# A two-layer hybrid trunk on one core: the MLP loop's two products interleaved matmul by matmul

## The reference

```python
    h = rms_norm(x, g_pre_mlp)
    y = jnp.square(jax.nn.relu(h @ w_mlp_in)) @ w_mlp_out
    return x + rms_norm(y, g_post_mlp)
```

## Time and profile before

| | before |
|---|---|
| median of 3 runs | 802.89 us (802.56 to 804.55) |
| the profiled execution's own time | 802.94 us |
| its span in the profile | 801.2 us |
| TensorE (PE) busy | 788.9 us, 98% |
| VectorE (DVE) busy | 505.4 us, 63% |
| ScalarE (ACT) busy | 403.0 us, 50% |
| DMA read from HBM | 144.31 MB, 181 GB/s over the span |
| TensorE's granted clock, mean | 0.996 |

### The profile page before, as it was taken

One profiled execution on the slowest core, in us unless ns is written; L12 is line 12 of the kernel. 1 busy time (PEld: TensorE's weight loads), 2 busy tenths in 40 slices (PEclk: granted clock), 3 DMA queues, 4 the chain that ended last, 5 costly groups with the idle time before them and its releaser, 6 DMA issues.

```text
span 801.2 us, 11130 instructions
## 1 busy us (share of the span) xinstructions
PE 788.9 (98%) x4126; PEld 664.5 (83%) x4126; DVE 505.4 (63%) x698; ACT 403.0 (50%) x619; POOL 56.7 (7%) x88
## 2 busy tenths in 40 slices
PE   8999999999999999999999999999999999999997
PEld 6898787887888888888879887878878888888885
DVE  4588555459777656556575776545687765655663
ACT  5565555444455454444555655655436654444441
POOL 2010000006110000000020100000242000000000
PEclk9999999999999999999999999999999999999999
DMA  7796455654467565666556864555644676666631
GB/s 243 208 295 212 125 158 158 197 181 147 132 203 226 179 187 190 193 201 204 173 150 192 277 198 122 154 180 179 205 138 131 198 219 186 184 205 190 180 128 53
DMA packets 85404, 145.87 MB, mean 182 GB/s; under 512 B 4950, under 2 KB 50406, under 8 KB 85367
## 3 DMA queue, kind: packets, MB, share of 16 engines
q1 hardware_dynamic: 85334, 145.33, 59.0%
q0 software_dynamic: 32, 0.05, 0.0%
HBM read 144.31 MB, written 1.05 MB: 181 GB/s over the span
## 4 chain that ended last, share of the span: by engine, by line
PE 90%; DVE 4%; POOL 2%; ACT 2%; DMA 1%; issue 1%; POOLq 0%; DVEq 0%; ACTq 0%
PE banks L1180 21%; PE banks L1182 21%; PE banks L1181 21%; PE banks L1228 11%; PE banks L1229 6%; DVE w_lo L730 2%; PE banks L1232 2%; DMA raw<-in_w_in_dram 1%; PE banks L1192 1%; PE banks L1231 1%; PE banks L1276 1%; PE banks L1294 1%; PE banks L1238 1%; PE banks L1268 1%; ACT w_hi L447 1%
## 5 line engine op out<-in xcount | busy, mean ns | idle before, releaser
L730 DVE TENSOR_TENSOR w_lo<-raw,w_hi 128x1024 fp32r<-128x1024 f32 (+1 forms) x272 | 317.3, 1196 | 126.1 <-ACT w_hi L447 125.5
L447 ACT CAST w_hi<-raw 128x1024 fp32r<-128x1024 f32 (+1 forms) x272 | 266.2, 1015 | 121.8 <-PE banks L1182 49.8
L1180 PE MATMUL banks<-w_hi,xT_both 128*128 128x512 f32 (+2 forms) x480 | 182.3, 380 | 0.8 <-DVE xT_both L753 0.8
L1182 PE MATMUL banks<-w_hi,xT_both 128*128 128x512 f32 (+2 forms) x480 | 178.1, 371 | 0.0
L1181 PE MATMUL banks<-w_lo,xT_both 128*128 128x512 f32 (+2 forms) x480 | 178.1, 371 | 0.0
L1228 PE MATMUL banks<-xT_both,w_hi 128*128 128x512 f32 x392 | 140.6, 398 | 0.0
L1180 PE MATMUL banks<-w_hi,brT_hi 128*128 128x512 f32 x320 | 125.0, 390 | 0.0
L1181 PE MATMUL banks<-w_lo,brT_hi 128*128 128x512 f32 x320 | 124.5, 389 | 0.0
L1182 PE MATMUL banks<-w_hi,brT_lo 128*128 128x512 f32 x320 | 124.5, 389 | 0.0
L1229 PE MATMUL banks<-xT_both,w_lo 128*128 128x256 f32 x392 | 110.0, 281 | 0.0
L1180 PEld LDWEIGHTS banks<-w_hi,xT_both 128*128 128x128 f32 x480 | 90.5, 189 | 17.9 <-issue 2.9
(11 more groups left out here) (176 smaller groups left out, 698.5 us busy)
## 6 DMA issues: line engine op xcount, KB each, us to landing
raw<-in_w_in_dram SPq DMA_DIRECT2D x96, 512.0 KB, 4.5
raw<-in_w_mlp_in_dram SPq DMA_DIRECT2D x64, 512.0 KB, 4.8
raw<-in_w_mlp_out_dram SPq DMA_DIRECT2D x64, 512.0 KB, 4.3
raw<-in_w_branch_dram SPq DMA_DIRECT2D x16, 512.0 KB, 4.0
raw<-in_w_out_dram SPq DMA_DIRECT2D x16, 512.0 KB, 3.8
raw<-in_w_in_dram SPq DMA_DIRECT2D x16, 176.0 KB, 3.2
x<-in_x_dram SPq DMA_DIRECT2D x4, 256.0 KB, 4.5
gain_pre<-in_g_pre_mlp_dram SPq DMA_DIRECT2D x2, 512.0 KB, 6.0
```

The costliest lines, as they stand in the source:

```text
L447: nc.scalar.copy(w_hi[:, c % RING, h * n:(h + 1) * n], raw[:, q % RAW, 0:n]).then_inc(hi_ready, 1)
L730: v.tensor_tensor(w_lo[:, c % RING, cut], raw[:, q % RAW, 0:n], w_hi[:, c % RING, cut].bitcast(F32), ALU.subtract).then_inc(lo_ready, 1)
L1180: nc.tensor.matmul(dst, l_hi, r_hi, start=first, stop=False)
L1182: return nc.tensor.matmul(dst, l_lo, r_hi, start=False, stop=last)
```

## The change

The loop calls a new function, `mlp_in_and_out`, in place of `mlp_in` and `mlp_out`. It waits for both chunks of the block and for the hidden part of step k at its beginning, and then issues the same 32 input matmuls and 24 output matmuls in turns: one output matmul between the wide and the narrow one of each kt, and another one behind every second kt. `chunk_used` is counted at the last input matmul, which is the last but one of the block, and at the last output matmul, the last of the block; before, the first count came at the end of the input product, in the middle of the block.

```diff
@@ -1524,6 +1524,46 @@
                             elif last:
                                 mm.then_inc(y_psum, 1)
 
+                def mlp_in_and_out(k_in, k_out, c, i):
+
+                    wait_chunk(l, c, i)
+                    wait_chunk(l, c + 1, i)
+                    pe.wait_ge(hidden_lo_ready, nth(l, STEPS, k_out + 2 * i))
+                    hi, lo = both(c)
+                    out_hi, out_lo = both(c + 1)
+
+                    def output_matmul(q):
+
+                        t, h, j, term = q // 12, q // 6 % 2, q // 3 % 2, q % 3
+                        n = hidden_slot(k_out) + j
+                        a = (brT_lo if term == 1 else brT_hi)[:, n, tokens(t)]
+                        w = (out_lo if term == 2 else out_hi)[:, j, columns(h)]
+                        return nc.tensor.matmul(psum[:, 2 * t + h, :], a, w, start=False, stop=False)
+
+                    q = 0
+                    for f in range(2):
+                        bank = 4 + 2 * (k_in % 2) + f
+                        cut = slice(f * P, (f + 1) * P)
+                        for kt in range(KT):
+                            wide = (psum[:, bank, :], hi[:, kt, cut], xT_both[:, kt, :, :].rearrange("p b n -> p (b n)"))
+                            narrow = (psum[:, bank, 0:S], lo[:, kt, cut], xT_hi[:, kt, :])
+                            if kt < KT - 1:
+                                nc.tensor.matmul(*wide, start=kt == 0, stop=False)
+                                output_matmul(q)
+                                nc.tensor.matmul(*narrow, start=False, stop=False)
+                            else:
+                                nc.tensor.matmul(*narrow, start=False, stop=False)
+                                output_matmul(q)
+                                last = nc.tensor.matmul(*wide, start=False, stop=True)
+                                if f == 1:
+                                    last.then_inc(chunk_used, 1)
+                            q += 1
+                            if kt % 2 == 1:
+                                mm = output_matmul(q)
+                                q += 1
+                    assert q == 24
+                    mm.then_inc(chunk_used, 1)
+
                 mlp_in(2, C_IN2, f=0)
                 hidden_transposes(l, 1)
                 mlp_in(2, C_IN2, f=1).then_inc(chunk_used, 1)
@@ -1532,8 +1572,7 @@
                     for b in range(2):
 
                         pe.wait_ge(relu_ready, nth(l, STEPS, 1 + b + 2 * i))
-                        mlp_in(3 + b, C_LOOP + 2 * b, i).then_inc(chunk_used, 1)
-                        mlp_out(1 + b, C_LOOP + 2 * b + 1, i)
+                        mlp_in_and_out(3 + b, 1 + b, C_LOOP + 2 * b, i)
                 pe.wait_ge(relu_ready, nth(l, STEPS, STEPS - 3))
                 mlp_in(STEPS - 1, CHUNKS - 4).then_inc(chunk_used, 1)
                 for t in range(T):
```

## The result

Twelve runs on one chip, six of each kernel: the changed kernel 806.74 us (806.23 to 809.09), before 803.55 us (802.56 to 804.55). The ratio is 1.0048, with a 95% interval of 1.0033 to 1.0062: about 3.9 us, between 2.7 and 5.0. Executions of either kernel fall into two groups some 2 us apart, three and three of before's, four and two of the changed kernel's, which is why the medians differ by only 3.2 us. The forecast was 804.7 us and "no change that can be told" (0.55); it came out on the slow side (0.33), inside the range of 801.0 to 809.0.

A forecast was written before the change was run, and what follows sets the result against it. TensorE was taken to bound the kernel, busy 788.9 of 801.2 us. To 802.94 us the forecast added 0 for matmul intervals, 0 for waits inside the loop and 1.8 for its end: 804.7 us, range 801.0 to 809.0.

The forecast's parts named there:

- no change that can be told: Whole kernel: time within about 0.3%, 2.4 us, of before, called "the same"; chance 0.55.
- Part 1: MLP loop: the number of wide, narrow and output matmuls per block stays as before; cost 0.
- Part 2: MLP loop: 14 steps from narrow to wide per block before and after, so the interval between matmuls stays; 0 us.
- The rule from the Trainium skill: MLP loop: loads and matmuls together set the spacing; output matmuls around narrow ones would remove the mixing price, 2.2 us less.
- Part 3: Inside the loop: earlier waits and later releases leave VectorE 2.9 us to spare per block; cost 0.
- Part 4: After each loop: the late split of chunk CHUNKS-2 makes TensorE wait on brT_lo; 0.9 us per layer, 1.8 in all.
- The sum: Whole kernel: 802.94 + 0 + 0 + 1.8 = 804.7 us, 0.2% above.
- alternating costs: Rival, every block: output matmuls amid the input product take up to 0.236 us, +5.4 us, 810.1 us; chance 0.24.
- The mixing price goes: Rival, in the loop: the queue hides the price of mixing widths, 2.2 us less, 802.5 us; chance 0.12.
- neighbours in other banks are cheaper: Rival, loop matmuls: half of about 13 ns per matmul goes, -9.0 us, 795.7 us; chance 0.12.
- the loop itself waits: Rival, each block: a wait for hidden part or chunk, 0.2 us a block giving 4.8, 809.5 us; chance 0.04.
- No wait at the end: Rival, behind the loop: ScalarE and VectorE overlap better than the rows, so no wait, 802.9 us; chance 0.08.

The follow-up runs named there:

- e1: Changed kernel's waits and releases, but matmuls in the order of before (32 input, then 24 output): ratio to before 1.0016, 1.3 us.
- e2: Changed kernel, but the loop's output matmuls read the input product's moving tile xT_both: layer 0's loop 134.23 us.
- e3: Changed kernel, but the loop's input matmuls write to the output's banks (0 to 3): layer 0's loop 134.23 us.
- e6: Changed kernel, but the loop's narrow matmuls are made 512 columns wide like the others: loop 152.33 us.
- e8: Changed kernel, but behind the loop ScalarE and VectorE do hidden part 14 ahead of and between the halves of chunk CHUNKS-2: 1.0031 of before, 2.5 us.
- e9_pairs: Before, but with the input product ordered two wide, two narrow, and so on: layer 0's loop 132.16 us.
- e4_grouped: Before, but each half of the input product has its 8 wide matmuls first, then its 8 narrow ones: ratio to before 0.9975, 2.0 us faster.
- e12: Changed kernel, but narrow matmuls in twos and hidden part 14 done first behind the loop: 1.0017 of before, loop 133.74 us.
- e7: Changed kernel, but each half's eight narrow matmuls together after wide and output ones in turns, both chunks given back at the last matmul: 1.0010 of before.

## Why the prediction was right or wrong

**Part 1, the counts**: right; 11130 instructions and 4126 matmuls in both profiles.

**Part 2, the interval between matmuls**: wrong, and this is the step that failed. It found the price of mixing widths, 0.09 us per block, took it for a constant of the step from narrow to wide, counted 14 steps before and 14 after, and put down 0. The count was right; the price per step went from 6.7 to 14.2 ns, because now two to five wide matmuls stand behind a step where before mostly one did. That is 0.106 us per block, 24 x 0.106 = 2.54 us. The trace of before held the warning. The wide matmul at 262.01 in the earlier trace rows was read as one at the plain pace, 0.23 us, from a single interval rounded to 0.01 us, when 0.01 us was the size in question. Averaged over the 12 blocks of layer 0's loop this interval is 0.236 us, longer than the 0.233 of the wide one ahead of it (0.24 in the rows), and behind the last narrow ones of a block a wide one takes 0.236 and the output matmul after it 0.233. The excess did not end with the first wide matmul, and the new order puts more of them behind a step.

**The rule from the Trainium skill** ("TensorE: Matmul & The Clock Gate", section "Back-to-back issue gap"): the page says that loads and matmuls together set the spacing. The forecast's own reading of it, that output matmuls around the narrow ones would take the mixing price away, had the wrong sign: 0.093 became 0.199 us. That a narrow matmul's surroundings count at all agrees with the rule; no run takes the loads and the matmuls apart.

**Part 3, waits inside the loop**: right. No wait inside either loop, and e1 shows that the bunched splits don't slow the matmuls. In the block that begins at 259.02 VectorE's last operation ends at 265.41 + 1.22 = 266.63, 7.6 us into it (8.2 forecast), which leaves 3.6 us to spare (2.9 forecast):

```profile
265.41 1.22 DVE L730 TENSOR_TENSOR w_lo<-raw,w_hi 128x1024 fp32r<-128x1024 f32 x1
```

**Part 4, the end of the loop**: right in place, cause and chain (`brT_lo` of hidden part 15 begins at 393.02, forecast 392.10 plus the loop's later end of 1.00). The size was 0.9 us per layer and measured 0.78 and 0.70. The hand-over from brT_hi to brT_lo took 1.08 us in part 14, as allowed for, but the next split of w_lo began where the chain had it without that (388.58, forecast 387.57 + 1.00), so it cost nothing.

**The sum**: 0 + 1.8 forecast, 2.54 + 1.48 = 4.02 us measured. The time is above the forecast's own range (804.3 to 805.4) and lies in the wide one (801.0 to 809.0) because that made room for the dearer alternation; the forecast itself had put nothing on what became almost two thirds of the difference, and a loop above 134 us was among its own signs of being wrong: it is 134.23. That is luck and no sign that the mechanism was understood. "No change that can be told" was set at 0.3%, and the whole interval of the ratio lies above it.

**The rivals**: "alternating costs" was the one that came true, at about half its price. Its working has a slip: (5.64 - 16 x 0.118) / 16 is 0.2345 us and not 0.236, which makes the worst case 4.5 us and not 5.4, 0.19 us per block against the 0.106 measured. Its mechanism was wrong: e2, e3 and e6 show that neither tile nor bank has a part. "The mixing price goes", "neighbours in other banks are cheaper" and "the loop itself waits" didn't come. "No wait at the end" needs another order of the queue, as in e8.

## What to carry to other kernels

When matmuls of two widths share a stream, look at the order of the widths before you interleave for any other reason. Here a step from narrow to wide cost 14 ns in the interleaved order and 20 with a long run of wide ones behind it, strict turns cost 6.7, and twos with twos or one long group per product almost nothing per block (e9_pairs; e4_grouped, faster than before by 0.25% and than the changed kernel by 0.7%). To find such a price in a trace, average an interval over all the blocks that repeat it. And when two buffers are given back together at the end of a loop body instead of one in the middle, walk the queues of the code behind the loop: the body had 3.6 us to spare and the tail had none, until its queue was put in another order.

## What was not expected of the hardware

- Uniform streams run at 0.22667 us for 512 columns, whatever the banks, moving and stationary tiles do from one matmul to the next (e6: 152.33 against 152.32 us), and at 0.1200 us for 256.
- In these runs the loops' length depends on the order of the widths alone and repeats to 0.01 us, in both layers and over four kernels that multiply different tiles (134.23, 134.23, 134.24, 134.23).
- The price of a step from narrow to wide is spread over up to five wide matmuls behind it (e4, e12).
- The spans do not repeat so well: the first transposes (L1192) began at 9.28 us in the profile of before and at 10.71 in that of e7, and the first loop at 248.11 and 250.12. These 2 us have nothing to do with the change. The 1.43 us at the transposes come from four matmuls ahead of them (L1378), which take 2.35 us in one trace and 3.78 in the other; why they do is open. That is why the loops were compared by their windows.
